# Retention on one core: weighing, rotations and closing product in another order, and scores and state kept in PSUM for their lower parts

## The reference, cut to what matters

```
h = rmsnorm(x, g_pre)
q, k, v, gate = split(h @ w_in)                      # 1024 x 6144
q, k = rope(q), rope(k) * 128 ** -0.5
scores = einsum(q_chunk, k_chunk) * inner_dec        # inner
o = scores @ v + (q @ R) * xi                        # R: carried state, 128 x 256 a head
R = R * g_c + (k * zeta).T @ v
o = (o - mean) * rsqrt(var + eps) * gn_gain
y = (silu(gate) * o) @ w_out                         # 1024 x 2048 @ 2048 x 1024
x_next = x + rmsnorm(y, g_post)
```

## Time and profile before

| | us |
|---|---|
| median of 3 runs | 2438.99 (2438.49 to 2439.3) |
| the profiled execution | 2435.32 |
| its span | 2433.5 |
| PE busy | 2376.3 (98%) |
| DVE busy | 1576.3 (65%) |
| ACT busy | 1054.4 (43%) |
| POOL busy | 854.8 (35%) |

### The profile page before, as it was taken

One profiled execution on the slowest core, in us unless ns is written; L12 is line 12 of the kernel. 1 busy time (PEld: TensorE's weight loads), 2 busy tenths in 40 slices (PEclk: granted clock), 3 DMA queues, 4 the chain that ended last, 5 costly groups with the idle time before them and its releaser, 6 DMA issues.

```text
span 2433.5 us, 33272 instructions
## 1 busy us (share of the span) xinstructions
PE 2376.3 (98%) x11720; PEld 2000.8 (82%) x11720; DVE 1576.3 (65%) x2621; ACT 1054.4 (43%) x1931; POOL 854.8 (35%) x874
## 2 busy tenths in 40 slices
PE   7999999998999999999999999999999999999998
PEld 6788888887788988888888888888888888888887
DVE  7767777776323421477765777677559776787785
ACT  6356555556312432555554554444343333333332
POOL 6576885775222311622221001001133323433112
PEclk9999999999999999999999999999999999999999
DMA  6444544445635223122334101112432434763422
GB/s 238 109 155 138 150 147 146 132 130 196 210 116 173 100 70 96 38 64 63 127 99 152 62 27 52 64 32 75 156 119 104 182 133 153 265 243 116 165 101 81
DMA packets 157450, 302.69 MB, mean 124 GB/s; under 512 B 13744, under 2 KB 83504, under 8 KB 155824
## 3 DMA queue, kind: packets, MB, share of 16 engines
q1 hardware_dynamic: 157296, 300.71, 36.9%
HBM read 207.33 MB, written 89.13 MB: 122 GB/s over the span
## 4 chain that ended last, share of the span: by engine, by line
PE 57%; DVE 4%; issue 2%; ACT 1%; DMA 0%; POOL 0%; DVEq 0%; SPq 0%; ACTq 0%; POOLq 0%
PE ff_ps L4379 11%; PE ff_ps L4406 11%; PE gl_vr_ps L3010 7%; PE wb_y_ps L3367 4%; PE gl_j_ps L2969 4%; PE la_x_ps L1804 4%; PE wc_y_ps L3748 3%; PE ff_ps L4437 2%; PE gl_l_ps L3036 1%; PE at_T_ps L2300 1%; DVE at_nmax L2176 1%; PE at_j_ps L2253 1%; PE at_v_ps L2254 1%; PE at_v_ps L2255 1%; PE at_v_ps L2253 1%
## 5 line engine op out<-in xcount | busy, mean ns | idle before, releaser
L4406 PE MATMUL ff_ps<-ff_p,ff_p 128*128 128x512 f32 x1176 | 268.1, 390 | 0.5 <-DVE ff_odd L4266 0.3
L4406 PEld LDWEIGHTS ff_ps<-ff_p,ff_p 128*128 128x128 f32 x1176 | 220.3, 188 | 48.3 <-issue 2.0
L2737 POOL TENSOR_SCALAR gl_mo<-gl_so 128x1 f32<-128x1 f32 x32 | 16.4, 512 | 332.7 <-ACT gl_osq L2675 332.7
L4025 ACT ACTIVATE ff_p<-ff_h 128x1024 fp32r<-128x1024 f32 x51 | 54.2, 1062 | 163.3 <-PE ff_ps L4406 163.3
L1343 DVE TENSOR_TENSOR ra_w_lower<-ra_b,ra_w_upper 128x1024 fp32r<-128x1024 f32 x59 | 89.8, 1523 | 45.7 <-ACT ra_w_upper L915 45.6
L538 PE MATMUL wa_y_ps<-wa_wh,wa_gl 128*128 128x512 f32 x256 | 104.4, 408 | 12.3 <-POOL wa_gl L504 6.8
L1598 PE MATMUL ra_even_ps<-ra_s_upper,ra_w_lower 128*128 128x512 f32 x264 | 106.8, 405 | 5.5 <-DVE ra_w_lower L1343 5.5
L4250 DVE TENSOR_TENSOR ff_p<-ff_h,ff_p 128x1024 fp32r<-128x1024 f32 x51 | 80.7, 1582 | 42.7 <-ACT ff_p L4025 42.7
L1598 PE MATMUL ra_even_ps<-ra_s_upper,ra_w_upper 128*128 128x512 f32 x264 | 104.0, 394 | 0.0
L1598 PE MATMUL ra_even_ps<-ra_s_lower,ra_w_upper 128*128 128x512 f32 x264 | 104.0, 394 | 0.0
L3010 PE MATMUL gl_vr_ps<-gl_vrh,x_lower 128*128 128x512 f32 x256 | 102.1, 399 | 0.0
(11 more groups left out here) (579 smaller groups left out, 7521.3 us busy)
## 6 DMA issues: line engine op xcount, KB each, us to landing
ff_h<-hidden SPq DMA_DIRECT2D x53, 512.0 KB, 3.3
ra_b<-in_w_chunks_a SPq DMA_DIRECT2D x47, 512.0 KB, 4.6
staging<-heads_a SPq DMA_DIRECT2D x64, 256.0 KB, 3.0
hidden<-ff_s SPq DMA_DIRECT2D x29, 512.0 KB, 2.8
ff_v<-in_w_ff SPq DMA_DIRECT2D x28, 512.0 KB, 6.8
ff_b<-in_w_ff SPq DMA_DIRECT2D x24, 512.0 KB, 5.7
hidden<-ff_a SPq DMA_DIRECT2D x24, 512.0 KB, 2.9
gated_a<-ra_oS SPq DMA_DIRECT2D x64, 128.0 KB, 2.7
```

The costliest lines, as they stand in the source:

```text
L4406: end = pe.matmul(to[:, u, :], a[:, k, i * P:(i + 1) * P], b[:, k, :], start=(opens and p < 3 and k == 0 and m == 0), stop=(k == 1 and m = ...
```

## The change

- **Opening (DVE, ACT).** The eight `weigh` of n = 3 come behind the `add` of that product, and go half by half (x21, x11, x21, x11). On ACT the square of the fourth block of rows (`square_x(3)`) comes ahead of `form_upper(s2)`.
- **Rotation of head 1 (DVE).** `scale_turns(1)` goes from n = 11 to 10, the first rotation from n = 12 to 11, `scale_turns(0)` stays at 12, and the second rotation is cut in three steps, at n = 13, 14 and 15.
- **Recurrence.** `sT` is written in PSUM, over the scores themselves, and the state in a PSUM bank of its own (`ra_R_ps`, before `ra_G_ps`). ACT copies it back to `R` in SBUF (48 times) ahead of `Rh`, since the next state is formed from `R` in SBUF. `kzl` on DVE waits until ACT has also made `sTh`, where before it waited for `vh`. NORM goes from 6 to 8, STORE from 7 to 9.
- **Closing product.** Transposes and products of the first two tiles lie at other slots and in other banks, and a slot has one row at most; ACT takes the row ahead of the gated tile; the last quarter (q = 3) of tiles 0 and 1 is multiplied by the gates that still lie in SBUF, which removes their DMA (`load_first_gates` with `rest`); `scale_gates` for C21 goes from slot 0 to 6 on POOL, its silu on ACT from slot 1 to 7; rows 6 to 9 have other places, all rows are asked for earlier, and rows 13 to 15 ahead of the gates of tile 2; the last tile's order is another.

```diff
-        ATTEND, DEVIATE, NORM, STORE = 3, 4, 6, 7
+        ATTEND, DEVIATE, NORM, STORE = 3, 4, 8, 9
...
-            g_first = core.enter_context(nc.psum_tensor("ra_G_ps", [P, HALF], F32))
+            state_ps = core.enter_context(nc.psum_tensor("ra_R_ps", [P, HALF], F32))
+            state = state_ps[:, 0:RV]
+            sT = [ts_ps[u][:, 3 * P:4 * P] for u in range(2)]
...
-        EARLY = {(FINAL, 8): ((0, 0),), (FINAL, 13): ((0, 1),), (CHUNKS, 0): ((0, 2),), (CHUNKS, 1): ((1, 0),), (CHUNKS, 2): ((1, 1),),
-                 (CHUNKS, 4): ((1, 2),), (CHUNKS, 5): ((0, 3),), (CHUNKS, 6): ((1, 3),)}
-        PRODUCT_AT = {(FINAL, 11): ((0, 0),), (FINAL, 13): ((0, 1),), (CHUNKS, 0): ((0, 2),), (CHUNKS, 1): ((1, 0),), (CHUNKS, 2): ((1, 1),),
-                      (CHUNKS, 4): ((1, 2),), (CHUNKS, 6): ((0, 3), (1, 3))}
+        EARLY = {(FINAL, 11): ((0, 0),), (FINAL, 13): ((0, 1),), (CHUNKS, 0): ((0, 2),), (CHUNKS, 1): ((1, 0),), (CHUNKS, 2): ((1, 1),),
+                 (CHUNKS, 3): ((1, 2),), (CHUNKS, 4): ((0, 3),), (CHUNKS, 5): ((1, 3),)}
...
+            if t < 2 and q == 3:
+                dve.wait_ge(post_done, 4 * GATES - 1)
+                for i, place_of in enumerate((C11, C12)):
+                    pair = slice(2 * i, 2 * i + 2)
+                    last = dve.tensor_tensor(first_sg[t][:, 12 + 2 * i:14 + 2 * i, :], ps[:, pair, :],
+                                             formed_even[place_of][:, :, t * P:(t + 1) * P], ALU.mult)
+                last.then_inc(prod_done, 1)
+                return
...
-            load_row(6)
-            load_row(7)
-            store_gates(FINAL, C12)
+                            load_row(6)
+                        if slot == 12:
+                            load_row(7)
             for kt in range(8, 11):
                 load_row(kt)
-            load_first_gates(0, 1)
-            load_first_gates(1, 1)
+            store_gates(FINAL, C12)
+            load_row(15)
             for slot in range(STORE):
                 core(CHUNKS, slot)
-            load_row(11)
-            load_row(12)
+            for kt in range(11, 15):
...
-                act.activation(vh[:, u, :], ts_ps[u][:, P:P + RV], ACT.Copy).then_inc(vh_done, 1)
-                act.activation(sTh[:, u, :], sT[:, u, :], ACT.Copy).then_inc(sTh_done, 1)
+                act.activation(vh[:, u, :], ts_ps[u][:, P:P + RV], ACT.Copy)
+                act.activation(sTh[:, u, :], sT[u], ACT.Copy).then_inc(sTh_done, 1)
...
-                    act.activation(Rh[:, :], R[:, :], ACT.Copy).then_inc(Rh_done, 1)
+                    if t < NT - 2:
+                        act.activation(R[:, :], state, ACT.Copy)
+                    act.activation(Rh[:, :], state, ACT.Copy).then_inc(Rh_done, 1)
...
+                for kt in ROWS_AT.get((c, slot), ()):
+                    row_upper(act, kt)
                 for at in PRODUCT_AT.get((c, slot), ()):
                     g_upper(act, *at)
-                for kt in ROWS_AT.get((c, slot), ()):
-                    row_upper(act, kt)
...
-                    form_upper(s2, x11, 4)
                     square_x(3)
+                    form_upper(s2, x11, (3, 5))
...
-                dve.scalar_tensor_tensor(sT[:, u, :], ts_ps[u][:, 3 * P:4 * P], xrms[:, 1, t:t + 1], decay[:, h % 2, :],
+                dve.scalar_tensor_tensor(sT[u], sT[u], xrms[:, 1, t:t + 1], decay[:, h % 2, :],
...
-                dve.wait_ge(vh_done, s + 1)
+                dve.wait_ge(sTh_done, s + 1)
...
-                dve.tensor_tensor(sTl[:, u, :], sT[:, u, :], sTh[:, u, :].bitcast(F32), ALU.subtract).then_inc(sT_done, 1)
+                dve.tensor_tensor(sTl[:, u, :], sT[u], sTh[:, u, :].bitcast(F32), ALU.subtract).then_inc(sT_done, 1)
...
-                        dve.scalar_tensor_tensor(R[:, :], R[:, :], carry[:, h:h + 1], ok_ps[:, RV:2 * RV],
+                        dve.scalar_tensor_tensor(state, R[:, :], carry[:, h:h + 1], ok_ps[:, RV:2 * RV],
...
-                    dve.tensor_tensor(Rl[:, :], R[:, :], Rh[:, :].bitcast(F32), ALU.subtract).then_inc(R_done, 1)
+                    dve.tensor_tensor(Rl[:, :], state, Rh[:, :].bitcast(F32), ALU.subtract).then_inc(R_done, 1)
...
+                if n == 10:
+                    scale_turns(1)
                 if n == 11:
+                    for step in range(3):
+                        rotate_odd(1, step)
+                if n == 12:
...
-                if n == 12:
-                    rotate_odd(1)
-                    scale_turns(0)
-                if n == 13:
-                    rotate_odd(0)
+                if 13 <= n < 16:
+                    rotate_odd(0, n - 13)
...
+                if n == 3:
+                    for half in range(2):
+                        dve.wait_ge(xg_done, half + 1)
+                        weigh(x21, x21, 0, x22, ALU.add, half)
+                        dve.wait_ge(xs_done, 2 * half + 2)
+                        weigh(x11, x11, 0, x21, ALU.subtract, half)
```

More of the change, by code:

```diff
@@ L410, in retention_and_latents @@
         sg_in = [sem(f"wa_sg_in{q}") for q in range(NQ)]
-        sg_first_in = [[sem(f"wa_sg_first_in{t}_{rest}") for rest in range(2)] for t in range(2)]
+        sg_first_in = [sem(f"wa_sg_first_in{t}") for t in range(2)]
         row_in = [sem(f"wa_row_in{i}") for i in range(8)]
@@ L505, in g_lower, with turning, turn_sines @@
                                ALU.subtract).then_inc(gl_done, 1)
-        def turn(eng, h, half, n, buffer, part, done):
+        def turning(h, half):
+            return formed_of(HEAD_CHUNKS[h])[(C12, C22)[half]], slice(half * HALF, (half + 1) * HALF)
+        def turn_sines(eng, h, half, buffer, part):
             c = HEAD_CHUNKS[h]
-            x_ = formed_of(c)[(C12, C22)[half]]
-            at = slice(half * HALF, (half + 1) * HALF)
+            x_, at = turning(h, half)
             if half:
@@ L517, in turn, with turn_cosines @@
             eng.tensor_tensor(buffer[:, 1, :], x_[:, 0, :], sin[:, at], ALU.mult).then_inc(part, 1)
+        def turn_cosines(eng, h, half, n, part):
+            x_, at = turning(h, half)
             eng.wait_ge(part, 3 * n + 1)
@@ L521, in turn, with turn_sums @@
             last.then_inc(part, 1)
+        def turn_sums(eng, h, half, n, buffer, part, done):
+            x_, _ = turning(h, half)
             eng.wait_ge(part, 3 * n + 2)
@@ L804, in load_gates @@
             def load_gates(t):
+                if t == NT // 2:
+                    wait_stored(sp, C22, FINAL)
                 for q in range(NQ):
@@ L1043, in _ @@
                     gates(FINAL, 2)
-                if slot == 1:
+                if slot == 7:
                     gates(FINAL, 3)
@@ L1200, in rotate @@
                     pool.wait_ge(odd_out[C21], 16)
-                turn(pool, h, half, n, turned_buffers[2 if h else 0], turn_part, turn_done)
+                buffer = turned_buffers[2 if h else 0]
+                turn_sines(pool, h, half, buffer, turn_part)
+                turn_cosines(pool, h, half, n, turn_part)
+                turn_sums(pool, h, half, n, buffer, turn_part, turn_done)
             def deviation(h, t):
@@ L1233, in _ @@
                 for slot in range(SLOTS if c < CHUNKS else TAIL):
-                    if slot == 0 and c - 1 in GATE_CHUNKS:
+                    if slot == (6 if c == CHUNKS else 0) and c - 1 in GATE_CHUNKS:
                         scale_gates(c - 1, 3)
@@ L1432, in _ @@
                     rows_lower(s3_sum, s3, 8, 0, (0, 4))
-                if n == 3:
-                    for half in range(2):
-                        dve.wait_ge(xg_done, half + 1)
-                        weigh(x21, x21, 0, x22, ALU.add, half)
-                    for half in range(2):
-                        dve.wait_ge(xs_done, half + 2)
-                        weigh(x11, x11, 0, x21, ALU.subtract, half)
                 if n == 4:
@@ L1445, in _ @@
                     for half in range(2):
-                        dve.wait_ge(xs_done, half + 4)
+                        dve.wait_ge(xs_done, 2 * half + 3)
                         weigh(x12, x12, 1, x11, ALU.add, half)
```

113 lines of the change are left out of this document (58 added, 55 removed).

## The result

The changed kernel took 2411.98 us in the median of 4 runs (2411.06 to 2417.33), beside 2438.74 of before (2436.34 to 2439.3): ratio 0.9895, 95% interval 0.9879 to 0.9911. The forecast was 2413.0. Taken once more, on the chip of the last four experiments, the same kernel gave 2415.75 (2414.78 to 2416.53) beside 2439.35: ratio 0.9905, 0.9888 to 0.9921. So the gain is 24 to 27 us, and a difference of under 4 us between kernels that did not share a chip says nothing.

A forecast was written before the change was run, and what follows sets the result against it. PE was taken as nearly always busy, bounded by five retention-layer waits totalling 27.2 us plus slowed clock. Terms 10.3 + 4.2 + 13.2 = 27.7, less 1.7, gave 26 us: 2439.0 - 26 = 2413.0, range 2407 to 2426.

The forecast's parts named there:

- the first two terms: Opening and rotation of head 1 together: 3.6 + 7.7 - 1.0 = 10.3 us gained, with ends 6 and 12.
- the others together: Recurrence, 4.2 us from the later normalisation, and closing product, 13.2 us from removed waits and the clock behind them.
- something else: Whole program: 1.7 us taken off the sum for short waits that a count does not see.
- The first step: Opening: PE starts the product needing `ra_s_lower` at 49.5 instead of 53.13, gaining 3.6 us.
- the upper end: Opening: if the first of the two halves is enough and arrives at 48.3, the gain is 4.8 us.
- I take 1 us off: Before the recurrence: deduction because PE may reach the first step before its tile, expected to land at 118 to 120.
- the clock's 2.2 us: Rotation of head 1: PE's time below full clock behind its 5.46 us wait, counted as regained with that wait.
- only half is cured: Rival: waits move to the first tile in the opening and row 12 in the closing; gain 16, 2423 us; chance 0.22.
- The PSUM moves at nothing: Recurrence: extra ACT copies and DVE waits, and quicker `Rl` and `sTl`, cost PE nothing; at worst 16 us.
- The short wait: Closing product: DVE falls back 0.5 us in slots 0 to 3, deducted from the gain there.
- Slower rival: Recurrence's output buffers: late stores hold ACT's output copy and PE, 36 us lost, 10 slower overall, 2449 us; chance 0.05.
- the margin of 3.5 us: Recurrence, store at slot 9: time left before the output buffer is rewritten, after store landing, normalisation and SP's queue.

The follow-up runs named there:

- the last four experiments: Changed kernel again, 2415.75 us; with POOL's first rotation waiting for DVE's, 2413.67; that wait plus values stored first, 2407.15; that wait plus scores and state in SBUF, 2415.21.
- the two edits on the kernel before: Opening's and rotation's edits, each alone on the kernel before: 2435.29 us (ratio 0.9993) and 2438.49 us (1.0005); both together 2435.49 us (0.9991).
- values first: Changed kernel with SP's stores of values of heads 0 and 1 ahead of the second half of rotated head 1: 2411.14 us, ratio 0.9888.
- the pair on one chip: Changed kernel with POOL's first rotation waiting for DVE's, 2413.67 us, against the same with values of heads 0 and 1 stored first, 2407.15 us.

## Why the prediction was right, and where it was not

**The total.** 26 us were forecast and 24 to 27 measured. It is right for most of its size, and by luck for the rest: the first two terms together were 5.1 us too high by the two traces (10.3 against 5.2) and 8 by the two edits on the kernel before, the others together some 2 us too low (17.4 against 19.2), I had taken off 1.7 for something else, and the first run fell at the good end.

**Opening.** The first step was wrong in size, 3.6 us against 6.3. I let PE wait for the end of both lower parts (49.5); it starts when the first half is there, which I had kept as the upper end with 4.8. The lower parts also start 1.7 us sooner than I held (45.47 for 47.16), because DVE was 0.6 us ahead and a lower part of the weights on its list took 1.21 us in place of 2.37. That the next wait of DVE's list would take the gain back I had not priced: the edit alone gives 6.9 us at that place, 3.6 at the first transposes and 2.4, not clear of noise, in the median.

**Rotation.** The wait on `ra_w_lower` goes as worked out, and PE reaches that product 11.8 us sooner (101.36 for 113.15). The step that failed is "I take 1 us off" for the tile: in place of 7.7 - 1.0 = 6.7 us the stage lost 1.1. What comes late next is a copy on ACT, whose place is freed by a store that stands in SP's queue behind the rotated head. I had followed that queue to the tile, and not asked who else waits for the stores on the way. PE stands 7.06 us behind it near 107, where I had forecast no wait, and the clock's 2.2 us that I had counted do not come, since the clock falls again (0.58, 0.73). With it gone (values first) the tile is the cap, at 4.1 us, so even then the 1 us was too little. The rival "only half is cured" named the chain of stores, at 6 us for both terms; 2 to 5 were measured.

**Recurrence.** 4.2 us were forecast for the later normalisation; in its stage 5.2 are gained, the 4.2 and 0.6 of the wait ahead of the closing product's first matmul (1.36 for 0.78), with the clock at 1.00 behind both waits of before. When it is undone 5.6 come back, 3.4 of waits and 1.5 of the clock. The rest of either, some half a us, is not explained. The PSUM moves at nothing: within a us and a half. DVE's busy time falls by 10.3 us on `Rl` and 17.8 on `sTl` (35.7 to 17.9 over all 64), together 28 where I had 24, and its waits grow by 9.5 ahead of `Rl` and 9.4 ahead of `kzl` (17.8 to 27.2), 19 where I had 40. Both effects are there, and hardly any of either reaches PE. DVE's rotation instructions, with two inputs in SBUF, take 1.8 us beside POOL and 0.69 without. The Trainium skill (SBUF — State Buffer, Who interferes with whom) has a DVE instruction with two inputs in SBUF contend with a GpSimd instruction that reads SBUF; these runs agree with it more plainly than the means I had.

**Closing product.** 13.2 forecast, 14.0 in its stage and 13.1 alone. The mechanism was the forecast one: waits of 10.95 us in that stage fell to 0.34, and the clock behind the two long ones, 0.70 from 610 to 615 us and 0.66 from 640 to 645 (4.67 x 0.34 = 1.6 us, where I had taken 1.4), is at 1.00. The short wait came at 0.34 us (0.5 forecast), the one at the start, which I had let stay, fell from 1.36 to 0.78, and PE waits for no row, although SP asks for rows 11 to 14 in one piece.

**Slower rival.** Its mechanism is real and begins between STORE = 9 and 11; the margin of 3.5 us at 9 was enough.

## What to carry to other kernels

Where a wait is removed early in a program, ask at the next shared end (here the stores ahead of the first tile) not only when its data come, but for each transfer on the way who reuses the buffer it frees, and what stands ahead of it in its queue. A queue that issues in fixed order passes one engine's lateness on to all whose transfers stand behind; moving two finished stores ahead of an unfinished one gave 6.5 us for no work, in the pair on one chip. And judge an undo of a few us on the same chip as the kernel it is to be compared with, by the stage in which the edit acts.

## What the runs showed that I had not expected

- The same kernel's median lay at 2411.98 and 2415.75 us on two occasions, with the kernel before at 2438.74 and 2439.35.
- A wait of 1.92 us on PE left the granted clock at 1.00 in one kernel, and one of 2.01 us at the same place of the program was followed by 0.87 and 0.78 in another.
- 49.3 us of ACT's waits for stores, in 36 pieces, cost PE 24 us, a part of it by the clock.
- DVE's two sums of a rotation took 1.4 us while POOL waited and 3.5 beside it, and POOL's wait of 3.3 us made the whole no slower.
